# Thirty throw-away identity products left out at three entries into a feed-forward network

## What is computed

```python
def first_block(...):                      # once
        x = x + 0.5 * swiglu(rms_norm(x, ffn1_norm[l]), ffn1_w_in[l], ffn1_w_out[l])
...
        x = x + mixed @ w_out[l]
        x = x + 0.5 * swiglu(rms_norm(x, ffn2_norm[l]), ffn2_w_in[l], ffn2_w_out[l])

def second_block(...):                     # two layers
        h = rms_norm_2(x, ffn1_norm_pre[l])
        x = x + 0.5 * rms_norm_2(swiglu_2(h, ffn1_w_in[l], ffn1_w_out[l]), ffn1_norm_post[l])
...
        x = x + rms_norm_2(y, mix_norm_post[l])
        h = rms_norm_2(x, ffn2_norm_pre[l])
        x = x + 0.5 * rms_norm_2(swiglu_2(h, ffn2_w_in[l], ffn2_w_out[l]), ffn2_norm_post[l])
```

## Time and profile before

| | |
|---|---|
| median of 3 runs | 1784.22 us (1783.42 to 1787.31) |
| the profiled execution | 1784.11 us, its span 1781.9 us |
| PE busy | 1757.3 us, 99% of the span |
| DVE, ACT, POOL busy | 61%, 52%, 2% |
| mean granted TensorE clock | 0.998 of full speed |
| chain that ended last | PE 95%, ACT 3%, DVE 1% |

### The profile page before, as it was taken

One profiled execution on the slowest core, in us unless ns is written; L12 is line 12 of the kernel. 1 busy time (PEld: TensorE's weight loads), 2 busy tenths in 40 slices (PEclk: granted clock), 3 DMA queues, 4 the chain that ended last, 5 costly groups with the idle time before them and its releaser, 6 DMA issues.

```text
span 1781.9 us, 31794 instructions
## 1 busy us (share of the span) xinstructions
PE 1757.3 (99%) x12924; PEld 1625.6 (91%) x12924; DVE 1090.2 (61%) x1457; ACT 920.6 (52%) x1218; POOL 36.3 (2%) x60
## 2 busy tenths in 40 slices
PE   8999998999999999999999999999999999999998
PEld 8999877999999999898899999999999898989997
DVE  6555776655565566566676555655574657675554
ACT  5444666444454445577755444544464577645443
POOL 0000220000000000000000000000000000000000
PEclk9999999999999999999999999999999999999999
DMA  7555523555555555453355555555555443446552
GB/s 308 201 191 189 186 95 120 216 201 194 205 206 195 192 179 192 182 192 119 135 184 191 189 188 196 199 199 200 191 198 176 178 171 119 152 155 222 192 188 95
DMA packets 46689, 324.34 MB, mean 182 GB/s; under 512 B 5392, under 2 KB 5648, under 8 KB 8464
## 3 DMA queue, kind: packets, MB, share of 16 engines
q1 hardware_dynamic: 44208, 315.81, 49.5%
q10 hardware_dynamic: 2400, 7.38, 1.1%
HBM read 322.12 MB, written 1.05 MB: 181 GB/s over the span
## 4 chain that ended last, share of the span: by engine, by line
PE 95%; ACT 3%; DVE 1%; issue 1%; DMA 0%; DVEq 0%; POOLq 0%; POOL 0%; ACTq 0%
PE work L1525 21%; PE work L1527 20%; PE work L1526 20%; PE acc L1527 8%; PE acc L1526 8%; PE acc L1525 8%; PE work L1579 4%; PE acc L1776 2%; PE acc L1758 1%; PE acc L1768 1%; ACT prob L731 1%; DVE lo L1011 1%; PE work L1626 0%; PE acc L1635 0%; ACT hi L610 0%
## 5 line engine op out<-in xcount | busy, mean ns | idle before, releaser
L1011 DVE TENSOR_TENSOR lo<-raw,hi 128x2048 fp32r<-128x2048 f32 x280 | 641.0, 2291 | 335.7 <-ACT hi L610 335.2
L1525 PE MATMUL work<-xT_hi,hi 128*128 128x256 f32 x2656 | 738.4, 278 | 1.2 <-DVE lo L1011 1.2
L610 ACT ACTIVATE hi<-raw 128x2048 fp32r<-128x2048 f32 x280 | 535.5, 1915 | 385.6 <-PE work L1527 353.5
L1527 PE MATMUL work<-xT_hi,lo 128*128 128x256 f32 x2656 | 734.4, 277 | 0.0
L1526 PE MATMUL work<-xT_lo,hi 128*128 128x256 f32 x2656 | 734.3, 276 | 0.0
L1525 PEld LDWEIGHTS work<-xT_hi,hi 128*128 128x128 f32 x2656 | 498.5, 188 | 10.5 <-issue 5.6
L1526 PEld LDWEIGHTS work<-xT_lo,hi 128*128 128x128 f32 x2656 | 499.3, 188 | 2.5
L1527 PEld LDWEIGHTS work<-xT_hi,lo 128*128 128x128 f32 x2656 | 498.6, 188 | 0.0
L1527 PE MATMUL acc<-hi,hT_lo 128*128 128x512 f32 x480 | 189.1, 394 | 0.0
L1526 PE MATMUL acc<-lo,hT_hi 128*128 128x512 f32 x480 | 188.2, 392 | 0.0
L1525 PE MATMUL acc<-hi,hT_hi 128*128 128x512 f32 x480 | 186.7, 389 | 0.0
(11 more groups left out here) (278 smaller groups left out, 2024.4 us busy)
## 6 DMA issues: line engine op xcount, KB each, us to landing
raw<-stream SPq DMA_DIRECT2D x298, 1024.0 KB, 4.8
mem_in<-mem ACTq DMA_DIRECT2D x3, 1024.0 KB, 6.2
post<-post ACTq DMA_DIRECT2D x6, 512.0 KB, 3.7
x<-x SPq DMA_DIRECT2D x2, 512.0 KB, 4.6
out<-x SPq DMA_DIRECT2D x4, 256.0 KB, 2.1
alibi<-alibi ACTq DMA_DIRECT2D x1, 768.0 KB, 10.3
params<-l_params SPq DMA_DIRECT2D x2, 328.0 KB, 5.5
params<-b_params SPq DMA_DIRECT2D x1, 534.0 KB, 10.0
```

Of the source, the lines that this page charges most:

```text
L610: nc.scalar.activation(hi[:, s, :], raw[:, s, :], ACT.Copy).then_inc(hi_ready, 1)
L1011: nc.vector.tensor_tensor(lo[:, s, :], raw[:, s, :], hi[:, s, :].bitcast(F32), ALU.subtract).then_inc(lo_ready, 1)
L1525: nc.tensor.matmul(dst, a_hi, b_hi, start=start, stop=False)
L1527: return nc.tensor.matmul(dst, a_lo, b_hi, start=False, stop=stop)
```

## The change

The three tens of the table become zeros:

```diff
-WAITING = {(None, 3): 0, (0, 0): 0, (0, 3): 10, (1, 0): 10, (1, 3): 10}
+WAITING = {(None, 3): 0, (0, 0): 0, (0, 3): 0, (1, 0): 0, (1, 3): 0}
```

## The result

The changed kernel takes 1788.09 us (median of 20 runs, 1782.48 to 1793.23), the kernel before in the same batch 1784.45 us (20 runs, 1783.27 to 1787.61). The ratio is 1.0019, 95% interval 1.0011 to 1.0028: some 3.4 us slower, clear of the noise of these runs. The spread is as telling as the median: the runs of before lie 4.3 us apart, those of the change 10.8 us, and its fastest run is 0.8 us faster than any of before.

What follows compares the result with a forecast made beforehand. PE's own work, busy 99% of the span, was taken as the bound. From 1784.1 us, 1.33 us gained at the entries and 2.4 us lost to clock falls gave +1.1, so 1785.2 us, range 1782.5 to 1788.3.

Steps and rivals of the forecast that it cites:

- The forecast case: At one or two of the three entries the clock falls: 1785.2 us, own range 1783.5 to 1787.0, chance 0.50.
- The gain: Transposes at (0, 3), (1, 0), (1, 3) start sooner after DVE without the products: 0.46 + 0.40 + 0.47 = 1.33 us.
- The new wait: PE waits some 1.6 us for DVE L1161 at each of the three entries, 4.5 to 5 us in total.
- The falls of the clock: Idle PE at each entry lowers the clock with chance about one half: 1.5 x 1.6 = 2.4 us lost on average.
- The price of 1.6 us: Cost of one fall, from nine 512-column products in the first block: 3.64 - 2.07 us; ends 0.7 and 2.1.
- the prediction's own sign: In the profile, a clock of 1.00 at all three entries, or 0.50 at all three, would make the forecast wrong.
- inside the FFNs PE all but never waits: PE, busy 99% of the span, bounds the kernel; what it gains or loses, nothing later takes back.
- the change also frees nothing else: At the entries, bank 0 of `work` is written anew by the first chunk anyway; the whole 1.33 us is on the path.
- could start at 947.89 to 947.97: At (0, 3), the last four transposes after the second column half (947.83), now at 948.17; not late for ACT.
- No fall: Rival: the clock falls at none of the three entries, only the gain is left: 1782.8 us, chance 0.19.
- The clock falls at all three: Rival: transposes don't hold up the clock, PE as good as idle 4.0 us at each entry: 1788.0 us, chance 0.23.
- The change does nothing: Rival: the wait at the entries only changes its name, gain near zero, clock unharmed: 1784.1 us, chance 0.08.

Runs made afterwards that it cites:

- the lucky trace: Trace of the profiled execution of the changed kernel (identity products at the three entries removed from the kernel before), the fastest of its 20 runs: 1782.48 us.

## Why the prediction was right or wrong

The forecast was 1785.2 us, a range of 1782.5 to 1788.3, and 0.83 on no change that can be told. Measured: 1788.09 us, a ratio of 1.0019, inside the range near its end and just within 0.2%, though a little over the 1787.8 us that the prediction had put as the border of slower. The forecast case's own range, 1783.5 to 1787.0, does not contain it. The stated range does, because it was widened for the rival with three falls, which did not happen. So that the number lay in the range was in part luck; the reasons held in part.

**The gain was right.** The prediction had 0.46, 0.40 and 0.47 us, 1.33 in all; POOL's rows give 0.45, 0.40 and 0.46, 1.31. The new wait is 4.7 us as foreseen (4.5 to 5). Nearly all of it reached the path: against the trace of before, POOL's rows of the lucky trace are 0.38 us early ahead of (0, 3) and 1.63 us early at the end, 1.25 us more.

**The falls of the clock were right in kind and price, and probably rarer than forecast.** Over the six traced kernels in which PE idled 1.6 us or more at the entries (18 entries) the clock fell at 6, where "a chance of about one half" at each has 9. The mean granted clock says the same: 0.9981 over the 31 runs of the change, 0.9989 over the 96 of before in the batches. A low stretch of 3.4 us takes 0.001 off, so the change added about one fall to a run (my estimate), not 1.5. The prediction took its half from the two idle times of one trace. All 14 traces have 21 idle times of 2.0 to 2.1 us in the first block, and the clock fell at the end of 8 of them or within 1.5 us behind it: five times, at 276 to 281 us, at the one that had left it alone in the trace of before, and three times at the other. With five, eight or nine products at the entries it fell at none of nine. The price of 1.6 us is about what the falls show: the first 32 products took 5.07 to 5.37 us in place of 3.72 or 3.85, some 1.2 to 1.6 us more. By the prediction's own sign, that a clock of 1.00 at all three places would speak against it, the profiled execution does so; the second trace of the changed kernel, with one fall, fits it.

**The missing term is the spacing of the products.** The step that failed is the one from "inside the FFNs PE all but never waits" and "the change also frees nothing else" to a sum with two terms, the gain and the falls: I took the duration of an FFN's products as given and put any change of it at nothing, without a reason. It isn't given. The same products run in 16.40 or in 16.82 us a trip, which of the two is settled by the FFN's second chunk, and the longer costs 4.3 to 4.6 us each time, three times a fall of the clock. In the traces it came at 8 of the 21 entries with a held second group of transposes. The prediction had seen that this group would have to wait ("could start at 947.89 to 947.97") and asked only whether it would be late for ACT. My worked-out sum with these rates would be -1.31 + 3 x 6/18 x 1.5 + 3 x 8/21 x 4.4 = +5.2 us; the means of the 20 runs each differ by 1788.3 - 1784.9 = +3.4 us, and those of the changed kernel run again by 1785.84 - 1785.27 = +0.6 us. So the two costs are enough for the loss, and their rates are known only roughly.

**The rivals.** *No fall* happened: it is the profiled execution, 1782.48 us where the rival had 1782.8; it is not the typical run. *The clock falls at all three* had the right size (1788.0) for the wrong reason; the run with transposes in place of the products excludes its premise, and no trace has falls at all three. *The change does nothing* is out. What I had not listed is a rival in which the work behind the wait runs slower at full clock; nothing in the trace of before shows the wide spacing in the FFNs. The run of 1787.31 us among the three of before may have had it: 17 of the 96 runs of before in the three batches lie at 1786.8 us or higher, 2 to 5 us over the medians, and the first FFN had the wide spacing in 3 of 14 traces.

What stays open is the mechanism of the two spacings. Shown is that they exist at full clock, that the choice lasts for the FFN, that the wide one costs what makes the slow runs slow, and that with the products as they were before none of the 96 runs is over 1790 us, where 5 of the 31 runs of the change are. That a held second group of transposes brings the wide spacing is not shown: in the traces it goes with it (8 of 21 entries, against none of 21 and none of 28), but a run of 1797.07 us of the kernel with both halves at once and one of 1791.74 us of the kernel with one product behind each wait need a wide FFN that this rule doesn't allow, and the program's first FFN has the wide spacing in 3 of 14 traces without such a group. Why the rhythm of later products shifts was not found.

## What to carry to other kernels

Work that fills a wait may pay for something other than the wait: here 2.2 us of throw-away work on PE cost 0.45 us at each place, kept the clock up and, more important, kept the wide spacing away from the FFN behind it. When a change makes one execution faster and the median slower, compare traces of several executions by an anchor that all have (here POOL's root instructions): the lateness appears where it arises, and here it lay over 170 us behind the edit in steps of 0.42 us. Fill a wait just past its end on each path (the traces speak for it, the times don't decide it), and check which wait the fill stands behind. And don't take a chance from two places of one trace: here it said one half and one place, and 14 traces say 8 of 21 and both places.

## What the runs showed of the hardware that I had not expected

- Streams of 128x128 by 256-column fp32r products have two spacings at a granted clock of 1.00: 0.1133 and 0.1177 us, each steady for an FFN of some 150 us and more; 512-column products keep 0.23 us.
- Transposes alone held the granted clock: 1.00 at three of three places with some 4.5 us of nothing else on PE.
- The granted clock fell at the end of or behind 8 of the 21 idle times of 2.0 to 2.1 us in the first block, behind 6 of the 18 of 1.6 us or more at the entries, and behind none of the three of 0.45 to 0.51 us. Every low stretch was 3.4 us long; at the entries each cost 1.2 to 1.6 us.
